# Gate sigmoids and the gated part move out of the ring, and the loads of three expert chunks move between mixing's weight pieces

## The reference, cut to what matters

```
gates = sigmoid(p_gate)                                 # [256, 2048]
mixed = gates[..., :D] * y_att + gates[..., D:] * y_rwkv
x = x + mixed @ w_out
x = x + hierarchical_moe(rms_norm(x), routers, w_expert_gate, w_expert_up, w_expert_down)
```

## Time and profile before

| what | value |
|---|---|
| median of 3 runs | 1357.8 us (1356.83 to 1359.24) |
| the profiled execution's own time | 1356.83 us |
| its span | 1355.0 us |
| TensorE busy | 1160.0 us, 86% |
| VectorE busy | 737.7 us, 54% |
| ScalarE busy | 487.1 us, 36% |
| DMA moved | 349.52 MB, mean 258 GB/s |
| mean granted TensorE clock | 0.939 |

### The profile page before, as it was taken

One profiled execution on the slowest core, in us unless ns is written; L12 is line 12 of the kernel. 1 busy time (PEld: TensorE's weight loads), 2 busy tenths in 40 slices (PEclk: granted clock), 3 DMA queues, 4 the chain that ended last, 5 costly groups with the idle time before them and its releaser, 6 DMA issues.

```text
span 1355.0 us, 22776 instructions
## 1 busy us (share of the span) xinstructions
PE 1160.0 (86%) x9669; PEld 919.5 (68%) x9669; DVE 737.7 (54%) x1120; ACT 487.1 (36%) x657; POOL 2.6 (0%) x11
## 2 busy tenths in 40 slices
PE   7999989997657366564739999999999999999998
PEld 6998778973213121221314998999998998999997
DVE  5487655852101010010104898877777899877776
ACT  4543435330000000000004546644446556644444
POOL 0000000000000000000000000000000000000000
PEclk9999999998878697788869999999999999999999
DMA  8842225999999999999999646566655436566650
GB/s 270 281 149 63 65 80 210 342 405 416 426 427 424 428 427 424 429 426 427 426 419 361 212 149 179 160 201 186 187 156 179 156 127 181 172 189 187 187 156 31
DMA packets 180986, 349.52 MB, mean 258 GB/s; under 512 B 8140, under 2 KB 154737, under 8 KB 167954
## 3 DMA queue, kind: packets, MB, share of 16 engines
q1 hardware_dynamic: 180394, 347.40, 70.6%
q10 hardware_dynamic: 488, 0.62, 0.2%
HBM read 346.93 MB, written 3.43 MB: 259 GB/s over the span
## 4 chain that ended last, share of the span: by engine, by line
PE 66%; DMA 17%; DVE 3%; issue 2%; SPq 1%; ACT 1%; DVEq 1%; ACTq 0%
PE ps L2868 25%; PE ps L2904 12%; DMA expert_ring<-in_w_expert_up 7%; PE ps L2058 6%; DMA expert_top<-in_w_expert_up 4%; PE ps L2089 4%; DMA expert_early<-in_w_expert_up 2%; DMA expert_ring<-in_w_expert_gate 2%; PE ps L225 2%; PE ps L2046 2%; PE ps L1708 2%; PE ps L2103 2%; PE ps L254 2%; PE ps L2880 2%; PE ps L2842 2%
## 5 line engine op out<-in xcount | busy, mean ns | idle before, releaser
L3216 DVE TENSOR_TENSOR w_lo<-expert_early,w_hi 128x2048 fp32r<-128x2048 f32 x80 | 182.8, 2291 | 25.7 <-ACT w_hi L3010 22.9
L2058 PE MATMUL ps<-expert_ring,w_slot 128*32 128x512 f32 x640 | 113.6, 712 | 96.7 <-DMA expert_ring<-in_w_expert_gate 40.9
L2131 DVE TENSOR_TENSOR hT<-ps,hT 128x512 f32<-128x512 f32 x8 | 8.5, 1068 | 340.9 <-PE ps L2058 340.9
L3010 ACT ACTIVATE w_hi<-expert_early 128x2048 fp32r<-128x2048 f32 x80 | 153.0, 1918 | 56.5 <-PE ps L2904 34.1
L2058 PEld LDWEIGHTS ps<-expert_ring,w_slot 128*32 128x32 f32 x640 | 30.3, 129 | 159.5 <-issue 159.5
L2868 PE MATMUL ps<-x_hi,w_hi 128*128 128x256 f32 x960 | 134.2, 282 | 0.0
L2868 PE MATMUL ps<-x_hi,w_lo 128*128 128x256 f32 x960 | 134.1, 282 | 0.0
L2868 PE MATMUL ps<-x_lo,w_hi 128*128 128x256 f32 x960 | 132.3, 280 | 0.0
L2868 PEld LDWEIGHTS ps<-x_hi,w_hi 128*128 128x128 f32 x960 | 122.9, 188 | 3.8 <-issue 1.6
L2868 PEld LDWEIGHTS ps<-x_hi,w_lo 128*128 128x128 f32 x960 | 123.0, 190 | 0.0
L2868 PEld LDWEIGHTS ps<-x_lo,w_hi 128*128 128x128 f32 x960 | 121.0, 188 | 0.0
(11 more groups left out here) (531 smaller groups left out, 2095.5 us busy)
## 6 DMA issues: line engine op xcount, KB each, us to landing
expert_ring<-in_w_expert_gate SPq DMA_DIRECT2D x22, 2048.0 KB, 29.4
expert_ring<-in_w_expert_up SPq DMA_DIRECT2D x18, 2048.0 KB, 29.3
expert_early<-in_ffn_up SPq DMA_DIRECT2D x36, 1024.0 KB, 6.0
expert_ring<-in_w_expert_down SPq DMA_DIRECT2D x14, 2048.0 KB, 29.8
w_slot<-in_w_in SPq DMA_DIRECT2D x26, 1024.0 KB, 5.5
expert_early<-in_w_in SPq DMA_DIRECT2D x20, 1024.0 KB, 5.5
expert_early<-in_ffn_down SPq DMA_DIRECT2D x18, 1024.0 KB, 4.9
expert_early<-in_w_expert_gate SPq DMA_DIRECT2D x6, 2048.0 KB, 26.9
```

The costliest lines, as they stand in the source:

```text
L2058: mm = pe.matmul(m.ps[rows_of(e), b, :], x_quad[:, k, rows_of(e)], w[e][:, k, :], start=(k == 0), stop=(k == KC - 1))
L3010: act.activation(w_hi[:, half_slot(l, i), :], raw_slot(m, i), ACT.Copy).then_inc(S["w_hi"], 1)
L3216: dve.tensor_tensor(w_lo[:, s, :], raw_slot(m, i), w_hi[:, s, :].bitcast(F32), ALU.subtract).then_inc(S["w_lo"], 1)
```

## The change

Four things change.

- The eight sigmoid places become `w_up`, `a_up`, the two of `g_up`, and four in `m.hT`. `sig_first` is no longer there (its 4 KB stay empty) and `rate` is no longer used for gates.
- `part` is two columns of `m.o_T` (the recurrence's output, which has been split into `branch_hi` and `branch_lo` by then), no longer at 76 KB of the ring.
- In `mix_sync`, piece 3 and chunk 3 go ahead of the router's loads, after `split_lo` 1. Chunk 4 goes between pieces 5 and 6, after the recurrence's branch has been multiplied.
- `APART` comes after piece 6 and waits for `gated` 2.

```
-    sig_first = sb("sig_first", [P, 2, 2, SEQ])
+    sb.at += 4 * KB
...
-    rate_sig = rate[:, :, :].rearrange("p (g f) n -> p g (f n)", g=2)
-    m.sig = [sig_first[:, 0, :, :], sig_first[:, 1, :, :], pair(m.w_up[:, :]), pair(m.a_up[:, :]),
-             pair(m.g_up[:, 0, :]), pair(m.g_up[:, 1, :]), pair(rate_sig[:, 0, :]), pair(rate_sig[:, 1, :])]
+    h_sig = m.hT[:, :, :].rearrange("p (g c) t -> p g c t", c=2)
+    m.sig = [pair(m.w_up[:, :]), pair(m.a_up[:, :]), pair(m.g_up[:, 0, :]), pair(m.g_up[:, 1, :])
+             ] + [h_sig[:, g, :, :] for g in range(GATES - WHOLE)]
...
-    part = room("gate_part", [P, 2, SEQ])
+    part = m.o_T[:, 0:2, :]
...
         load_expert_chunk(sp, m, a, 2)
         load_rows(sp, m, a, 0)
+        sp.wait_ge(split_lo, 1)
+        load_mix_piece(sp, m, a, RING)
+        load_expert_chunk(sp, m, a, 3)
         sp.wait_ge(branch_lo_done, 2)
...
-        for i in range(RING, MIX_PIECES):
+        for i in range(RING + 1, MIX_PIECES):
             sp.wait_ge(split_lo, i - RING + 1)
             load_mix_piece(sp, m, a, i)
             if i == RING + 1:
                 sp.wait_ge(m.gate_done, 2 * GATES)
                 load_expert_chunk(sp, m, a, TOP)
+            if i == RING + 2:
+                await_filled(sp, ("rwkv", 3))
+                load_expert_chunk(sp, m, a, 4)
+        sp.wait_ge(gated, 2)
+        load_expert_chunk(sp, m, a, APART)
...
-        for g in (3, 4, APART, 5, 6, 7):
-            if g == 3:
-                sp.wait_ge(gated, 4)
+        for g in (5, 6, 7):
             if g == 5:
                 await_filled(sp, ("out", 2, 1))
```

## The result

The changed kernel takes 1361.8 us (median of 7 runs, 1361.34 to 1363.30) against 1357.8 us (median of 7, 1356.83 to 1359.24). The ratio is 1.003, with a 95% interval of 1.002 to 1.0041: slower by some 4 us, outside the predicted range of 1355.3 to 1361.0. Its profiled execution took 1361.34 us and has a span of 1359.5 us.

The account below looks back on a forecast made before the run. Mixing was taken as bound by TensorE and the experts' stage as a DMA byte stream; + 0.6 us (mixing) - 0.9 us (chunk 6) = - 0.3 us gave 1357.5 us, range 1355.3 to 1361 us.

Parts of the forecast that it names:

- The idle time of 247 to 252 us is filled: - 2.8 us: Landing of piece 5: chunk 3 ahead adds 4.9 us, filled DMA idle time takes off 2.8 us, so 270.0 us.
- The DMA engines have work all that time, so I cost the stalls at 0: SyncE's issues behind piece 3: chunk 3 stalls to about 247 us, later loads wait for room, cost 0.
- My bound of 1.4 us from `TOP`: SyncE's stalls, if their cover fails: up to 1.4 us, from the 1.39 us by which `TOP`'s issue was held.
- Mixing + 0.6 us: End of mixing: late low halves of pieces 5 and 6 make it 0.6 us later, bounds 0 and 3.1.
- Mixing pays for the chunks: Rival, in mixing: `w_out` pieces stand behind chunks 3 and 4 and stalled issues; + 2.2 to + 3.6 us, say 1361; 20%.
- Chunk 6 from 9.1 to 8.2 us, - 0.9: Ahead of the first quarters: the head start shortens chunk 6's time from issue to landing, worth 0.9 us, bounds 0 and 3.1.
- The overhang goes: Rival, at the first quarters: they start 3.1 us sooner on the slowest DMA engines; 1355.3 us; 13%.
- The change doesn't do what it says: Rival, in SyncE's queue: chunks 3 and 4 get no head start, neither term is there; 1357.8 us; 10%.
- the new homes at 0: VectorE and ScalarE: same instructions and shapes at other addresses, taken as 0, under 0.5 us either way.
- piece 3's earlier issue at 0: SyncE's queue: piece 3 may go at 241.1 instead of 250.38 us, but TensorE isn't waiting for it; worth 0.
- chunk 3 held until about 247 us: Sign of being right, on SyncE: chunk 3's issue stalls behind piece 3's 1024 elements to about 247 us.
- the dip of the share just before chunk 6: Sign of being right, in the DMA share: a dip just before 288 us, as the queue idles before 286.42.

Follow-up runs that it names:

- the staged kernel: The changed kernel with the router's five loads issued at about 200 us into the empty 4 KB, then copied by ScalarE: 1358.63 us, ratio 1.0001.
- the sigmoid late on ScalarE: The changed kernel with the router's five small loads issued by ScalarE in place of SyncE: 1367.92 us, ratio 1.007.
- the nine matmuls that outlast the wait: The changed kernel with nine extra 128x512 matmuls on TensorE ahead of `out(2)`: 1366.96 us, ratio 1.0057.
- the two staged kernels: The staged kernel and the staged best order, both with the router's loads issued early: 1358.63 us and 1358.50 us.
- the staged best order: New homes, pieces 3 to 5 ahead of chunk 3, one row quarter before chunk 5, router's loads issued early into the empty 4 KB: 1358.50 us, ratio 0.9999.
- the kernel with chunk 3 late: The changed kernel with chunk 3 sent behind piece 6, chunk 4 still between pieces 5 and 6: 1357.51 us, ratio 0.9995.

## Why the prediction was wrong

Seven kernels, the one before among them, have no wait for a split in mixing and take 72.10 to 72.13 us from chunk 0 to the first quarter. The other seven take 75.68 us or more. Two of these lose by their own edit: the sigmoid late on ScalarE, and the nine matmuls that outlast the wait. In the other five the time at which piece 5 lands decides, counted from chunk 0's issue: 38.3 us in before and 39.5 us in the staged kernel are in time, 42.5 us in after, and 42.4 to 43.4 us in the other four, are not. The forecast was 270.0 - 229.62 = 40.4 us, just in time.

- **"The idle time of 247 to 252 us is filled: - 2.8 us"** is the step that failed. The share there did go to 1.11, as predicted, but 2.5 us of idle time came back at 255 to 259 us. The idle time was never a lack of loads that one more chunk could fill. It belongs to the stretch in which SyncE stands at the router's small loads with nothing long behind, and goes where they go; the staged kernel and the two with these loads ahead of chunk 2 show it. Piece 5 at 272.1 instead of 270.0 us is this term.
- **"The DMA engines have work all that time, so I cost the stalls at 0"**: wrong for the same reason. I had thought that chunk 3 takes the stall over ("now chunk 3 is what stalls") and that the router's loads then pass. They don't: from the issue of the first vector to the end of the five they keep SyncE from 240.50 to 250.38 us before, 9.9 us, and from 246.44 to 256.81 us in after, 10.4 us. Chunk 3's own 5.21 us came on top. The queue ran dry at about 255 us, with chunk 3 nearly through and SyncE still held until 256.3 us. My bound of 1.4 us from `TOP` was too low: the nearest row was not that one but the 6.61 us itself, once more.
- **Mixing + 0.6 us**: measured + 3.76 us. The working was sound, but its landings were wrong. With piece 5 at 272.1 us it gives 2.0 + 0.4 = 2.4 us. Piece 6 landed at 280.7 instead of 278.0 us on before's scale; its high half is then ready at 282.6 us, and with that the same working gives 3.1 + 0.4 = 3.5 us. What it had no term for is the clock behind the wait: with two extra matmuls the clock stays up and `out(2)` takes 6.2 in place of 7.3 us, but then piece 6 and the low halves take what was gained. The slow clock and piece 6 stand side by side, so they don't add.
- **Rival "Mixing pays for the chunks"**, 20%, 1361 us, is what happened, by its mechanism: one wait of 2.0 us and a half clock in place of "3 to 4 us of waits". Its point of decision, piece 5 after 272.8 us, was too late; 272.1 was enough.
- **Chunk 6 from 9.1 to 8.2 us, - 0.9**: the size was right (8.1 us), the worth was not. Chunk 6 was not what the stream waits for; the two staged kernels have 8.2 and 8.1 us for chunk 6 and gain nothing. This step failed too, with nothing lost by it here but 0.9 us of the sum.
- **Rival "The overhang goes"**: refuted by the staged best order, where it does go (3.1 to 0.2 us) and the time stays.
- **Rival "The change doesn't do what it says"**: refuted. Chunk 3 lands at 257.8 us on before's scale, where the kernel before issues it at 265.62 us. The head start is there and is worth nothing.
- Right were: the new homes at 0; piece 3's earlier issue at 0 (it stays early in the kernel with chunk 3 late); chunk 3 held until about 247 us (245.6, 246.8 on before's scale); the dip of the share just before chunk 6 (0.31 at 287 to 290 us); and that from the first quarter on nothing changes (a share of 1.01).

In sum: 3.76 us before the first quarter, where - 0.3 was forecast. The rest of the kernel takes 1053.1 to 1055.7 us from there in the 14 profiled executions, without an order that follows the edits. The 0.3 us between 3.76 and the 4.0 of the medians are inside this scatter.

## What to carry to other kernels

An idle stretch of a DMA queue has an owner. Before counting on filling it, look at which load was being issued or moved in it. If it belongs to loads in many small elements, it may move with them, as here; sending them when the queue had little to do took it away. And a head start for the loads behind a stage is worth nothing where the stage's end, and not the queue, releases the next loads. Ask both questions ahead of moving 2 MB past a piece whose slack is 1.7 us.

## What the runs showed of the hardware

- An issue that follows a load in 1024 elements can be held, whichever of the two engines issues it: 5.21, 6.30 and 5.42 us on SyncE in after, 5.33 us on ScalarE. It isn't always: behind pieces 3 and 4 in the kernel before, right after the hole, the issue of `TOP` took only 1.39 us. With the loads on ScalarE a sigmoid came 10.06 us late.
- Around the router's five loads, some 2,400 packets of 16 to 128 bytes, the 16 DMA engines were idle for about 2.5 us in a stretch of 4 us (58 GB/s) in after, for 2.8 us in the kernel before, and for 2.0 us with chunk 3 late (a share of 0.34 at 252 to 255 us). Sent from ScalarE beside chunk 3 the same loads left no such hole (shares of 1.18 and 1.07 from 247 to 260 us).
- A load does not fill the engines at the moment of its issue. In after piece 4 goes at 256.81 us; the share is still 0.18 from 257 to 258 and 0.61 from 258 to 259 us. An estimate from these slices is that 1.4 of the 2.5 us of the hole stand behind that issue.
- A wait of TensorE of 2.0 to 2.5 us ahead of `out(2)` was followed, 0.3 to 1.0 us after it ended, by 3.4 us at 0.50. With waits of 0.7 and 1.6 us (router's loads ahead of chunk 2), or 1.0 us behind two extra matmuls, the clock stayed at 1.00.
- From the issue of chunk 0 to that of the first quarter the seven kernels without a wait take the same time to 0.03 us, while their whole profiled executions range from 1356.0 to 1359.5 us. To size an edit of under 0.3%, measure its stretch.
